# A hybrid recurrent trunk: first tiles of a layer evicted in place, the residual stored in quarters, row groups placed anew

## The reference

```python
for li in range(2):
    xn = rmsnorm(h, norm_g[li])
    if li % 2 == 0:   # "ab": gated DeltaNet (8 heads) || GLA (4 heads)
        u = xn @ ab_w_in; qkv = silu(causal_conv4(qkv)); beta = sigmoid(.)
        g = -exp(a_log) * softplus(a + dt_bias)          # one row per head
        y = concat(o_dn * silu(z), o_gla * silu(z)) @ ab_w_out
    else:             # "cd": Mamba-2 SSD (16 heads, 4 groups) || RG-LRU
        u = xn @ cd_w_in; xbc = silu(causal_conv4(xbc) + bias)
        g = -exp(a_log) * softplus(dt_in + dt_bias)      # one row per head
        y = concat(y_ssd, y_lru) @ cd_w_out
    h = h + y
    h = h + sigmoid(rmsnorm(h, ple_norm) @ ple_w_gate[li]) * (p[li] @ ple_w_proj[li])
return rmsnorm(h, final_norm), new states
```

## Time and profile before

| | us |
| --- | --- |
| median of 3 runs (2649.93 to 2665.92) | 2650.56 |
| the profiled execution | 2650.76 |
| its span, first to last instruction | 2648.9 |
| mean granted clock of TensorE | 0.969 |

### The profile page before, as it was taken

How to read it: one execution, slowest core, us unless ns; L and a number is a source line. 1 busy time by engine, 2 the same in 40 slices (tenths; PEclk the granted TensorE clock), 3 DMA queues, 4 the chain that set the end, 5 groups by cost and what they waited for, 6 DMA issues and landing times.

```text
span 2648.9 us, 51461 instructions
## 1 busy us (share of the span) xinstructions
PE 2485.6 (94%) x22813; PEld 2339.3 (88%) x22813; DVE 1212.5 (46%) x1982; ACT 919.8 (35%) x1215; POOL 407.4 (15%) x584
## 2 busy tenths in 40 slices
PE   8899999999999999899999998999999969999996
PEld 7898888888889998789999988888889969998996
DVE  6553554535544553532243344466545553233332
ACT  5413343233333344332232241333335453233222
POOL 2101011110100101011111111122212212111111
PEclk9999999999999999999999999999999979999998
DMA  9333333233333544543333333443444445333322
GB/s 241 107 92 91 99 99 100 84 91 91 103 107 99 153 140 116 161 158 88 88 88 89 88 128 98 111 115 112 119 120 122 137 126 161 88 87 83 87 79 77
DMA packets 378862, 292.94 MB, mean 111 GB/s; under 512 B 20295, under 2 KB 342609, under 8 KB 378104
## 3 DMA queue, kind: packets, MB, share of 16 engines
q1 hardware_dynamic: 336272, 172.51, 24.0%
q0 software_dynamic: 24944, 83.64, 9.8%
q10 hardware_dynamic: 17424, 33.50, 3.5%
HBM read 231.10 MB, written 59.23 MB: 110 GB/s over the span
## 4 chain that ended last, share of the span: by engine, by line
PE 78%; DVE 7%; ACT 6%; DMA 4%; issue 4%; POOL 0%; ACTq 0%; SPq 0%; DVEq 0%; POOLq 0%
PE psd L541 62%; PE psw L564 2%; PE psw L563 2%; PE psw L584 1%; DVE w_lo L1634 1%; ACT w_hi L1099 1%; PE psw L612 1%; PE psw L569 1%; PE psw L634 1%; DVE arena L1735 1%; DMA w_raw<-in_ab_w_in_dram 1%; DMA raws<-uT_scratch 1%; DMA uT_scratch<-mix 1%; PE psw L620 1%; DMA mix<-in_x_prompt_dram 1%
## 5 line engine op out<-in xcount | busy, mean ns | idle before, releaser
L541 PE MATMUL psd<-xh,w_hi 128*128 128x272 f32 x5056 | 1118.7, 303 | 46.7 <-DVE xl L1686 13.4
L541 PE MATMUL psd<-xh,w_lo 128*128 128x272 f32 x5056 | 1055.6, 290 | 2.0 <-issue 2.0
L541 PE MATMUL psd<-xl,w_hi 128*128 128x272 f32 x5056 | 1054.9, 290 | 0.5 <-issue 0.5
L541 PEld LDWEIGHTS psd<-xh,w_hi 128*128 128x128 f32 x5056 | 805.3, 191 | 107.6 <-issue 45.6
L541 PEld LDWEIGHTS psd<-xl,w_hi 128*128 128x128 f32 x5056 | 806.3, 191 | 0.0
L541 PEld LDWEIGHTS psd<-xh,w_lo 128*128 128x128 f32 x5056 | 801.3, 191 | 2.7 <-issue 2.7
L1634 DVE TENSOR_TENSOR w_lo<-w_raw,w_hi 128x1024 fp32r<-128x1024 f32 x316 | 388.3, 1231 | 583.6 <-ACT w_hi L1099 582.1
L1099 ACT CAST w_hi<-w_raw 128x1024 fp32r<-128x1024 f32 x316 | 328.8, 1043 | 772.9 <-PE psd L541 741.5
L2445 POOL TENSOR_TENSOR states<-states,extra 128x544 f32<-128x544 f32 x59 | 98.5, 1670 | 562.9 <-ACT extra L1154 562.9
L2386 POOL DMA_DIRECT2D raws<-uT_scratch x61 | 38.1, 625 | 775.9 <-DMA uT_scratch<-mix 686.4
L2267 DVE TENSOR_TENSOR extra<-psd,rstd 128x544 f32<-128x544 f32 x32 | 23.2, 724 | 143.2 <-PE psd L541 112.7
(11 more groups left out here) (499 smaller groups left out, 2331.4 us busy)
## 6 DMA issues: line engine op xcount, KB each, us to landing
w_raw<-in_ab_w_in_dram SPq DMA_DIRECT2D x112, 512.0 KB, 4.0
w_raw<-in_cd_w_in_dram SPq DMA_DIRECT2D x74, 512.0 KB, 4.1
w_raw<-in_ple_w_gate_dram SPq DMA_DIRECT2D x64, 512.0 KB, 3.9
uT_scratch<-mix ACTq DMA_DIRECT2D x92, 272.0 KB, 4.3
w_raw<-in_ab_w_out_dram SPq DMA_DIRECT2D x32, 512.0 KB, 3.9
w_raw<-in_cd_w_out_dram SPq DMA_DIRECT2D x32, 512.0 KB, 3.9
raws<-uT_scratch POOLq DMA_DIRECT2D x40, 272.0 KB, 3.1
hT_scratch<-arena POOLq DMA_DIRECT2D x2, 4352.0 KB, 19.0
```

The source lines that it names most:

```text
L541: mm = pe.matmul(out[:, D0 + HALF * half:D0 + HALF * (half + 1)], w[:, r, k % KH, :], x[:, k, HALF * half:HALF * (half + 1)], start=(k == ...
```

## The change

Six things are done together.

1. The x tiles of DeltaNet head 0 (tiles 0, 2, 3) and the four of bc are DIRECT: VectorE evicts them to `raws`, and convolves each on its own right after (direct_tile). They are no longer staged, stored and loaded. POOL's sample_rows waits for the eviction. bc is convolved and activated in two pairs. The DeltaNet history, which lay in `raws`, is loaded in three pieces elsewhere.
2. In VectorE's fill the eviction stands at slice 16k, ahead of that slice's split; before it stood at 16k + 1, behind it.
3. store_h stores a quarter. The first four go out as the x are ready; of the second four, three go out during gate0 and one at its end.
4. Row groups: VectorE's steps are spread by fills at 12, 15 and 19 slices after the start, ln stands behind the exp of a_log on ScalarE, the working rows use slots 4 to 10. c0 of ab comes 28 slices after the row tile (before: 44), in cd eg and c0 come 30 and 36 after (before: 34 and 68).
5. The group eg of cd, 16 small matmuls, becomes one of 192 columns, whose operand VectorE makes.
6. The norms: gate0 and gate1 at SL + 3 (before: 2SL), cd at SL - 1 (before: 2SL); g0 at SL + 12 (before: 2SL), and its wait for the copies of p stands right before it.

```diff
-                if u[0] == "ab_rows":
-                    end = SL * (max(RAW[("dn", 0), "x"]) + 1) + 12
+                if u[0] in ("ab_rows", "cd_rows"):
+                    end = last + (28 if u[0] == "ab_rows" else 36)
...
             def evacuate(d):
...
+                if d in DIRECT:
+                    dst = raws[:, T * DIRECT[d]:T * DIRECT[d] + T]
...
                     n = at[0]
+                    if n % SL == 0 and evac[0] < n // SL:
+                        evacuate(n // SL - 1)
                     for q in SPLITS.get(n, []):
                         split_lo(q)
-                    if n % SL == 1 and evac[0] < n // SL:
-                        evacuate(n // SL - 1)
...
+            def direct_tile(u, i, wcol, bcol, done):
+
+                d = RAW[u, "x"][i]
+                fill(SL * (d + 1) + 2)
+                dve.wait_ge(S[f"dense_read{d % 2}"], d // 2 + 1)
+                for tap in range(TAPS):
+                    conv_tap((i,), tap, False, wcol, bcol, slot, done)
...
             def rows_ab():
-                fill(SL * (ROWS["ab"] + 1) + 2)
-                dve.wait_ge(S["h_stored"], 16)
-                go(dve.memset(slot(0), 0.0))
+                base = SL * (ROWS["ab"] + 1) + 2
+                fill(base)
+                dve.wait_ge(S["h_stored"], 64)
+                go(dve.memset(slot(4), 0.0))
                 go(dve.memset(slot(11), 0.0))
+                direct_tile(("dn", 0), 0, lambda i, w: pvc("dn_conv_w", 24 * w + 8 * i), None, S["dn_conv"])
...
             def bc():
-                fill(target[u, "start"])
-                dve.wait_ge(S["u_loaded"], loads[u])
-                dve.wait_ge(S["rows_copied"], 3)
-                conv(4, lambda i, w: pvc("ssd_conv_w", 12 * w + 8 + i), lambda i: pvc("ssd_conv_b", 8 + i), slot,
-                     smp_of[u], S["bc_conv"])
...
+                for pair in (0, 1):
+                    tiles = (2 * pair, 2 * pair + 1)
+                    for i in tiles:
+                        direct_tile(u, i, weight, bias, S["bc_conv"])
+                    dve.wait_ge(S["smp_ready"], smp_of[u] - 1 + pair)
+                    for tap in range(TAPS):
+                        conv_tap(tiles, tap, True, weight, bias, slot, S["bc_conv"])
...
-            fill(first_slice("gate0") + 2 * SL)
+            fill(first_slice("gate0") + SL + 3)
             norm(1)
             gate(0)
-            fill(first_slice("cd") + 2 * SL)
+            fill(first_slice("cd") + SL - 1)
             norm(2)
...
-                    for h in range(SSD_H):
-                        mm = pe.matmul(W[:, 12 * h:12 * h + 12], ident[0:SSD_H, h:h + 1].broadcast_to([SSD_H, P]),
-                                  small[0:SSD_H, 16:28], start=True, stop=True)
+                    pe.matmul(W[:, 0:SSD_H * 12], ones[0:SSD_H, :], slot(11)[0:SSD_H, 0:SSD_H * 12], start=True,
+                              stop=True).then_inc(S["work_ready"], 1)
...
-            def store_h(i):
-                pool.wait_ge(S["x_ready"], KT * (1 if i == 0 else 4))
-                pool.dma_start(hD.rearrange("c p t -> p c t"), arena3).then_inc(S["h_stored"], 16)
+            def store_h(q):
+                pool.dma_start(hD[4 * q:4 * q + 4].rearrange("c p t -> p c t"), arena3[:, 4 * q:4 * q + 4])\
+                    .then_inc(S["h_stored"], 16)
...
+                    if layer == 0 and c % 4 == 1 and c > 4:
+                        pool.wait_ge(S["gate_done"], c - 1)
+                        store_h(c // 4 - 1)
...
-            store_h(0)
+            for q in range(4):
+                pool.wait_ge(S["x_ready"], 4 * q + 4)
+                store_h(q)
...
-            store_h(1)
+            pool.wait_ge(S["gate_done"], KT)
+            store_h(3)
```

More of the change, by code:

```diff
@@ L336, in trunk @@
                 RAW.setdefault((t[4], t[5]), []).append(d)
+        DIRECT = {d: i for u in (("dn", 0), ("bc", 0)) for i, d in enumerate(RAW[u, "x"])}
         staged = {}
         for units in (UNITS, UNITS_CD):
-            tiles = [d for u in units for part in "xvz" for d in RAW.get((u, part), [])]
+            tiles = [d for u in units for part in "xvz" for d in RAW.get((u, part), []) if d not in DIRECT]
             for i, d in enumerate(tiles):
@@ L440, in trunk @@
         for u in UNITS + UNITS_CD:
-            if (u, "x") in RAW:
+            if (u, "x") in RAW and RAW[u, "x"][0] not in DIRECT:
                 n += 16
@@ L1077, in _ @@
                     tail(u, (8, 4, 8), (24, 32, 36), (27, 27, 36))
-            fill(first_slice("gate1") + 2 * SL)
+            fill(first_slice("gate1") + SL + 3)
             norm(3)
@@ L1849, in rows_cd @@
                 split_rows(rowG[H, :], 0, SSD_H).then_inc(S["rows_split"], 1)
             def dn_conv(h, tap, samples=False):
-                steps = range(tap, TAPS) if h == 0 else (tap,)
-                for tap in steps:
-                    if h == 0 and not samples:
-                        fill(target[("dn", 0), "start"] + 2 * tap + 2)
-                    conv_tap(3, tap, samples, lambda i, w: pvc("dn_conv_w", 24 * w + 8 * i + h), None, slot, S["dn_conv"])
+                conv_tap(range(3), tap, samples, lambda i, w: pvc("dn_conv_w", 24 * w + 8 * i + h), None, slot, S["dn_conv"])
```

154 lines of the change are left out of this document (91 added, 63 removed).

## The result

The changed kernel takes 2593.41 us (median of 4 runs, 2590.28 to 2594.62). The kernel before takes 2654.16 us in the runs beside it (4 runs, 2649.93 to 2665.92). The ratio is 0.9761, interval 0.9742 to 0.9779: 2.4% faster, some 61 us. The forecast was 2602 with a range of 2594 to 2615, so the direction was right and the forecast gain was too small, by a fifth: 49 us against 61 between the medians (56.1 between the two profiled spans). Later runs make the miss larger. Executed again on another occasion, the same two kernels gave 2588.33 and 2657.95 us.

The account below looks back on a forecast made before the run. PE, busy 94% of the span, was taken as the bound. Gains of 10.9 (front of ab), 5 (heads), 8.2 (gate stages) and 24.9 (front of cd) summed to 49 us off 2650.76: 2602 us, 80% range 2594 to 2615.

Parts of the forecast that it names:

- Heads of ab: DeltaNet heads 3, 4, 5: eviction ahead of the split frees ScalarE at tile stores; 3 x 1.9 us, 5 taken.
- Rival 3: GLA and SSD units: earlier evictions release ScalarE there too, 5 us at most; 2597 or below, chance 0.10.
- Front of ab: Start of ab: waits for tile 2's eviction and head 0's squares go, less new c0 and ssq waits; 10.9 us net.
- Gate stages: gate0 and gate1: earlier norms and g0 remove two 2.15 us waits, 1.0 for w_lo and 2.9 of clock; 8.2 us.
- Front of cd: Start of cd: earlier norm, quarter stores, single eg matmul and no trip or block remove waits and clock loss; 24.9 us.
- norm 2: Front of cd: norm 17 slices sooner removes the 5.60 us eviction wait and 2.3 us of clock.
- (1): Front of ab gives gain back: c0 waits 3.0 us, ssq 2, each with half clock; 2608, chance 0.2.
- (2): Whole kernel: waits shorten but 8 of 11 us clock gains appear elsewhere, heads give nothing; 2615, chance 0.12.
- (4): All 94 evictions delay a split PE needs, 0.718 us each, adding 67.5 us; 2669, slower than before, chance 0.03.

Follow-up runs that it names:

- experiment 6: a_evict_late with finished tiles' stores issued at slice 16k + 12 instead of 16k + 3 between slices 240 and 544; 2627.03 us, 0.9877 of the kernel before.
- a_evict_late: Changed kernel with VectorE's eviction behind the split again, at slice 16k + 1; 2612.48 us, 0.9837 of the kernel before.
- experiment 3: The run a_evict_late: changed kernel with the eviction behind the split again; 2612.48 us, 0.9837 of the kernel before.
- experiment 12: Changed kernel with POOL's SSD selector made before its store and load waits, and g0 at SL + 8; 2578.25 us, 0.9705 of the kernel before.
- experiment 7: Changed kernel with both gate stages' norm matmuls, transposes and g0 back at 2SL; 2599.61 us, 0.9784 of the kernel before.
- a_same: Changed kernel executed again with no edit; 2588.33 us, 0.9745 of the kernel before.

## Why the prediction missed

**The step that failed is "Heads of ab"**, with its sentence that the swap costs nothing where DVE is waited for by nobody, and 5 us for it in all. That the swap gains was right, and how it gains was right for head 3 (experiment 6). The size was not: 19 to 24 us in the changed kernel, 30 in the kernel before. It failed in three ways.

First, I counted the waits at one kind of place, heads 3, 4 and 5. The eviction stands in front of the chains that start from a finished tile, and those are in other stages too: c0 in ab, the last SSD pair, the output of cd. In slices 1616 to 2064 the swap is worth 8 to 10 us in the changed kernel; through which chain was not tested. Rival 3 named this, with "5 us at most" because the waits listed there were few. They were: the listed idle of PE is 112.0 us in a_evict_late and 105.6 and 102.6 in the two executions of the changed kernel, so 6 to 9 us.

Second, in the three heads that I did count, I added up 3 x 1.9 us without asking which wait ends last behind the released ScalarE. Idle time there fell by 1.8 us and not by 5, because in head 4 a wait for VectorE took the place of those that went.

Third, I gave the clock only to the waits over 2 us, and nothing to the small ones. PE is not busy for 6 and 9 us less than in a_evict_late, but the spans differ by 17 and 25: the larger half is busy time at a higher clock. In slices 256 to 544 some 3 us less idle time came with 5.9 us less busy time (means of the two lists in experiment 3: 359.5 and 353.6). I did not read the clock in those windows before predicting; at 0.98 over 384 us it was there to be seen. That the small waits bring the lower clock is not shown as such: in experiment 6 the same window had 10.8 us more idle time and only 1.4 more busy time, and experiment 12 had 357.2 us of busy time with the waits as short as in the changed kernel. What is shown is that the two lists differ.

**The other terms together were right.** Without the swap the changed kernel is at 0.9837 (0.9819 to 0.9855), 43 us below the 2657 us of the kernel before. My other terms sum to 44. Singly they were off by a few us either way. By term:
- Front of ab: 10.9 forecast, 13.2 up to slice 160. c0 waits 1.3 us (1.5) and ssq 0 (0.5). 6.2 us are idle time; the other 7.1 are less busy time for the same 1708 records, so clock, for which I had 1.6 + 1.1. 4 us were lost again in slices 160 to 256, which is chance: the second execution did not lose them. The c0 wait is shorter because of the swap (0.9 to 1.9 us in six executions with it, 3.0 to 3.4 in three without).
- Gate stages: 8.2 forecast, 9.2 in the traces, 7.5 by undoing it. The idle part was right. I had put 2.9 us of clock in gate1. In slices 2290 to 2320 PE is busy for 34.8 to 35.3 us in all four executions that start from the kernel before, and with the new placing 31.8 or 31.9 in four and 33.3 or 33.4 in four; undoing the placing alone (experiment 7) gave 33.4. So the row was not the luck of one execution, and the new placing wins the clock only part of the time. The Trainium skill's free-running window (TensorE: Matmul & The Clock Gate, Part 1) agrees with the 31.8 and 33.4 of two executions of one kernel, but does not explain why all four that start from the kernel before lie at 34.8 or more.
- Front of cd: 24.9 forecast, 26.9 in the traces. Undoing norm 2 gives 7.6 (5.6 + 2.3 = 7.9 forecast). The quarters were needed: without them 7 us come back. eg is 6.2 and not 3.5.

**Rivals.** (1) The front gave nothing back. (2) "The clock is not won" was wrong in sign: more clock was won than I had counted (10.1 us in the terms, which the rival rounds to 11). I had raised the high end for it and left the low end at 2594. (3) Nearest to what happened, too small. (4) No split was late: in the changed kernel PE waits for w_lo 0.9 us in all, and 2.0 without the swap. It did not decide because VectorE idles before the splits.

**Numbers.** The sum was set against one execution of 2650.76 us; the kernel's runs have medians of 2656 to 2658 later, so this execution was some 7 us better than usual. A median of three did not show that. Set against 2657 the same sum gives 2608, 15 to 20 us above what the changed kernel takes: that the forecast missed by only 8.6 us is luck, since two errors partly cancel.

## What to carry to other kernels

When two instructions on a lightly loaded engine become ready at the same moment, order them by who is waiting for the results and not by their length; ask this of every stage, not only of those with a long wait in the list. When a wait is removed, ask which one ends next behind it: here 1.90 us appeared where 0.36 had been. Where a stretch stands at 0.98 of the clock instead of 1.00, removing small waits can gain more than their idle time (here about three times, once), so a sum over waits needs the clock of the window beside it. One profiled execution is one draw: compare it with the spread of the times before a term of 5 us is called safe.

## What the runs showed of the hardware

- The clock fell behind the 32 small eg records with PE busy 8.00 of 8.00 us: a pair of dense matmuls started every 0.45 us instead of every 0.25 from 1567.3 to 1572.9, and the window 1568:1576 stands at 0.69, so a part at 1.2 of 2.4 GHz. One matmul in their place thus gave 6.2 us, not their own 3.4.
- In slices 256 to 544 the clock largely followed the program (six executions against eight, though the highest of the eight, 357.2 us, comes within 0.3 of the lowest of the six), while in slices 128 to 256 and 880 to 960 the same kernel had 0.96 and 0.99, and 0.89 and 0.92.
- A store of h in quarters took a median of 10.7 us to landing when spread out (10.2 in a_same) and 13.6 when the four were issued together; the whole had taken 16.3 to 21.8.
